# A decoder block with 64 experts: list entries spread over partitions, one weight load issued later, and one PSUM copy moved from ScalarE to VectorE

## What is computed

```python
g_idx = argmax(hn @ w_group + b_group)             # one group of 8
top_l, top_i = top_k(e_logits_of_group, 2)         # two of its 8 experts
w = softmax(top_l) * g_prob[g_idx]
# for each token t and each of its two experts e = g_idx * 8 + top_i:
hb = silu(hn[t] @ w_gate[e]) * (hn[t] @ w_up[e])   # 1024 -> 256
out[t] += w * (hb @ w_down[e])                     # 256 -> 1024
```

## Time and profile before

| | us |
|---|---|
| timed runs | 2643.99, 2638.89, 2644.9 |
| profiled execution | 2639.34 |
| its span | 2637.7 |
| TensorE busy | 2459.3 (93%) |
| VectorE busy | 1841.3 (70%) |
| ScalarE busy | 1049.5 (40%) |
| GpSimd busy | 518.3 (20%) |
| experts' stage, from its table load to the end | 1895.9 to 2637.7 |

### The profile page before, as it was taken

How to read it: one execution, slowest core, us unless ns; L and a number is a source line. 1 busy time by engine, 2 the same in 40 slices (tenths; PEclk the granted TensorE clock), 3 DMA queues, 4 the chain that set the end, 5 groups by cost and what they waited for, 6 DMA issues and landing times. The chain is left out here.

```text
span 2637.7 us, 33454 instructions
## 1 busy us (share of the span) xinstructions
PE 2459.3 (93%) x12296; PEld 2006.0 (76%) x12296; DVE 1841.3 (70%) x2387; ACT 1049.5 (40%) x1516; POOL 518.3 (20%) x474
## 2 busy tenths in 40 slices
PE   6999999999999999999995997999399999999998
PEld 6899888999877878889884775778277777766664
DVE  7699998677211068888886775466578888877773
ACT  5101101444212158788774221233255555544440
POOL 1222222111101101111110000011424443332221
PEclk9999999999999999999997998999699999999999
DMA  5111212223324153354424775546479999998886
GB/s 170 40 56 56 73 51 86 78 91 116 108 97 121 48 147 98 98 156 115 119 81 126 205 228 167 201 155 228 155 278 363 366 374 360 359 352 340 340 315 206
DMA packets 180271, 469.84 MB, mean 178 GB/s; under 512 B 33573, under 2 KB 104579, under 8 KB 145548
## 3 DMA queue, kind: packets, MB, share of 16 engines
q1 hardware_dynamic: 133202, 371.64, 41.3%
q0 software_dynamic: 31120, 49.48, 5.5%
q10 hardware_dynamic: 15794, 46.67, 4.6%
HBM read 408.65 MB, written 118.29 MB: 200 GB/s over the span
## 5 line engine op out<-in xcount | busy, mean ns | idle before, releaser
L92 PE MATMUL project_bank<-project_xnT_hi,project_w_hi 128*128 128x512 f32 (+4 forms) x1352 | 512.9, 379 | 0.8 <-DVE project_work L775 0.7
L93 PE MATMUL project_bank<-project_xnT_lo,project_w_hi 128*128 128x512 f32 (+4 forms) x1352 | 499.9, 370 | 0.0
L94 PE MATMUL project_bank<-project_xnT_hi,project_w_lo 128*128 128x512 f32 (+4 forms) x1352 | 497.7, 368 | 0.0
L788 DVE SCALAR_TENSOR_TENSOR project_work<-project_work,project_taps 128x2048 f32<-128x2048 f32 x128 | 335.3, 2620 | 4.5
L92 PEld LDWEIGHTS project_bank<-project_xnT_hi,project_w_hi 128*128 128x128 f32 (+1 forms) x1352 | 252.1, 186 | 36.7 <-issue 8.3
L93 PEld LDWEIGHTS project_bank<-project_xnT_lo,project_w_hi 128*128 128x128 f32 (+1 forms) x1352 | 252.2, 187 | 33.2 <-issue 6.8
L94 PEld LDWEIGHTS project_bank<-project_xnT_hi,project_w_lo 128*128 128x128 f32 (+1 forms) x1352 | 252.3, 187 | 27.2 <-issue 0.6
L2633 PE MATMUL experts_y_bank<-weights_down,experts_hT 128*128 128x512 f32 x544 | 246.9, 596 | 19.4 <-DMA weights_down<-in_w_down_dram 18.7
L1265 DVE TENSOR_TENSOR attend_pT<-attend_t_bank,attend_pT 128x512 fp32r<-128x512 f32 (+3 forms) x352 | 213.8, 613 | 33.7 <-ACT attend_pT L1199 32.7
L1132 PE MATMUL attend_o_bank<-attend_pT,attend_values 128*128 128x256 f32 x1216 | 225.0, 304 | 6.7 <-DVE attend_pT L1265 6.7
L1199 ACT ACTIVATE attend_pT<-attend_t_bank 128x512 fp32r<-128x512 f32 (+3 forms) x352 | 184.7, 540 | 86.9 <-PE attend_t_bank L1118 84.2
(11 more groups left out here) (311 smaller groups left out, 4620.7 us busy)
## 6 DMA issues: line engine op xcount, KB each, us to landing
weights_down<-in_w_down_dram SPq DMA_DIRECT2D x68, 1024.0 KB, 20.9
weights_gate_up<-in_w_gate_dram SPq DMA_DIRECT2D x45, 1024.0 KB, 7.2
weights_gate_up<-in_w_up_dram SPq DMA_DIRECT2D x45, 1024.0 KB, 18.8
weights_third<-in_w_gate_dram SPq DMA_DIRECT2D x23, 1024.0 KB, 7.1
weights_third<-in_w_up_dram SPq DMA_DIRECT2D x23, 1024.0 KB, 17.7
project_w_raw<-in_w_in_dram SPq DMA_DIRECT2D x36, 512.0 KB, 4.1
qk_d<-project_work SPq DMA_DIRECT2D x16, 1032.0 KB, 5.6
gate_d<-project_work ACTq DMA_DIRECT2D x16, 1024.0 KB, 4.1
```

The lines of the kernel that those rows point to most:

```text
L92: pe.matmul(out, lhs[0], rhs[0], start=first, stop=False)
L93: pe.matmul(out, lhs[0], rhs[1], start=False, stop=False)
L94: return pe.matmul(out, lhs[1], rhs[0], start=False, stop=last)
L788: nc.vector.scalar_tensor_tensor(out=work[:, 2, 0:SEQ], in0=work[:, 1, META - 1 + q:META - 1 + q + SEQ], scalar=taps[:, bass.ds(ct, 1), q] ...
```

## The change

It has three parts.

1. The table's entries are laid over the partitions in another order, both in the table load and in the loads of the further jobs' lists. Entry r went to partition r; now it goes to partition (r mod 16) x 8 + floor(r / 16). A list of 43 tokens, which filled partitions 0 to 42, now fills two or three partitions of each group of eight.
2. Gate and up of job 3 are no longer loaded at the end of route, but at the start of the experts' stage, behind the first gather and ahead of job 4's.
3. In the steps of jobs 0 to 61 `take_hidden` moves from ScalarE, where it stood between the halves of `split_high`, to VectorE, where it stands behind `scale_rows` and ahead of both halves of `split_low`. Job 62 and the jobs behind it keep it on ScalarE.

```diff
@@ stage_route, SyncE
             first_weights.load_down(sp, room_of(2), expert_of(2))
-            wait(sp, first_weights.low_ready, 4 + 2)
-            first_weights.load_gate_up(sp, 0, expert_of(3))
             for s in stored:
@@ stage_experts
+        def spread(entries):
+            return entries.rearrange("(b a) e o -> a b e o", a=16)
@@ SyncE
-            sp.dma_start(table[:, :, :], table_rows[0:P, :, :]).then_inc(table_loaded, 16)
+            sp.dma_start(table[:, :, :], spread(table_rows[0:P, :, :])).then_inc(table_loaded, 16)
@@ SyncE, load_list
-                sp.dma_start(columns[:, j + 1:j + 2, :], table_rows[bass.ds(first, P), bass.ds(n, 1), :],
+                sp.dma_start(columns[:, j + 1:j + 2, :], spread(table_rows[bass.ds(first, P), bass.ds(n, 1), :]),
@@ SyncE
             wait(sp, rows_loaded[room_of(0)], 16)
+            load_gate_up(3)
             load_gate_up(4)
@@ ScalarE, step
-                if before >= 1:
-                    take_hidden(n - 1, 1 - b)
-                if n >= 1 and after >= 1:
                     high_gate_up(n + 1, 1 - b, q + b, 1)
@@ VectorE
+            def take_hidden(n, b):
+                wait(dve, hidden_turned, n + 3)
+                wait(dve, down_done, n + 1)
+                nc.vector.tensor_copy(hT[:, b, :, :], gu_bank[:, b, 0:DE].rearrange("p (c t) -> p c t", t=P))\
+                  .then_inc(hT_ready, 1)
@@ VectorE, step, behind lower_x and scale_rows
+                if before >= 1:
+                    take_hidden(n - 1, 1 - b)
+                if after >= 1:
                     if n >= 1:
                         lower_gate_up(n + 1, 1 - b, 0)
                         lower_gate_up(n + 1, 1 - b, 1)
```

## The result

| | before | changed kernel |
|---|---|---|
| median of the runs, us | 2642.91 (2638.89 to 2644.9, 4 runs) | 2626.56 (2626.27 to 2628.89, 4 runs) |
| profiled execution, us | 2639.34 | 2628.89 |
| its span, us | 2637.7 | 2627.3 |

The ratio of the times is 0.9939, 95% interval 0.9924 to 0.9955: 16 us faster, 12 to 20. A second timing of the changed kernel, on another chip, gave 2629.54 us and a ratio of 0.9949 (0.9932 to 0.9966).

A forecast was written before the change was run, and what follows sets the result against it. TensorE, then late the fullest DMA engine, was taken as the bound. -14.0 (order), 0 (load) and +1.0 (copy) gave -13.0 us, execution 2626.3; with the runs' median offset 2631, so the middle, 2628.5, was named; range 2614 to 2644.

The forecast's parts named there:

- The bound: Experts' stage: TensorE sets the pace for some 40 jobs, then the fullest DMA engine; 18.7 us of TensorE waits.
- The dealing in fours: List gathers and scatters: engine j takes partitions 4j to 4j + 3 and 32 + 4j to 35 + 4j.
- Rival A: Lists' rows are dealt in eights, so the new order levels all engines and 18.7 us go: 2618 to 2625; chance 0.10.
- B: Experts' stage: memory's rate, not the DMA engines, is the limit, so time stays at 2639 to 2644; chance 0.16.
- the term of the sum, 5.1 us left to show: Experts' stage: after the new order, 20.3 us of backlog less 15.2 hidden by the loads' lead leave 5.1 us.
- The prediction's own lower case: Job-by-job tally of the experts' stage with weights at 7.4 us: 6.6 us of waits left, gain 12.
- the 14.0 of the term: Experts' stage: gain in us from the new entry order, TensorE's 18.7 us of waits falling to 4.7.
- Rival D: Start of the experts' stage: job 3's weights come late, 5 us given back, 2633; chance 0.04.
- The forecast of 1 us: Late steps: the copy of `hT` on VectorE delays the down product by 1.1 us, paid once; 1 us loss.
- rival C: VectorE's queue: `hT` waits behind a scatter's buffer and a gather, 1.1 us in each of 21 late steps: 2650; chance 0.12.
- What would show it: Signs: down-weight waits about 5 us from near job 50, scatter landing 8 to 9 us, seven or eight engines ending job 5's gather.
- T: Experts' stage: rows dealt in fours, the fullest engine builds a backlog, costing TensorE time once the loads' lead is used up.

The follow-up runs named there:

- level: Kernel before, table loaded by four DMAs so that list entry r goes to DMA engine r mod 16 by the map in fours: 2610.9 us, ratio 0.9874.
- packed: Kernel before, table loaded by four DMAs so that each DMA engine gets eight neighbouring list entries before the next gets any: 2661.33 us, ratio 1.0065.
- level_late: Kernel before, with only the lists of jobs 32 to 63 dealt entry r to engine r mod 16: 2615.74 us, ratio 0.9895.
- load_only: Kernel before, with only job 3's gate and up load moved into the experts' stage: 2645.84 us, ratio 1.0000.
- copy_only: Kernel before, with only the copy of `hT` moved from ScalarE to VectorE behind `scale_rows`: 2642.51 us, ratio 0.9998.
- no_copy: Changed kernel with the copy of `hT` back on ScalarE, keeping the new entry order and the later load: 2628.38 us, ratio 0.9932.
- level_early: Kernel before, with only the lists of jobs 0 to 31 dealt entry r to engine r mod 16: 2632.35 us, ratio 0.9958.
- level_all: `level` plus job 3's load in the experts' stage and the copy of `hT` on VectorE: 2611.26 us, ratio 0.9876.

## Why the prediction was right

**The bound.** Right. TensorE sets the pace up to some point, the fullest DMA engine behind it. That the engine is full, and neither memory nor the order of instructions, is shown by `level` and `packed`, which differ in nothing but the partition, and with it the engine, that each row goes to. No run tells the engine apart from something else that its group of partitions might share.

**The dealing in fours.** Right, and shown three times: by the gather of 43 rows at 0.41 and at 0.88, by `level` with no wait left, and by `packed` with 32.1 us. Rival A is dead with it: in eights, the changed kernel would have had no waits. The Trainium skill ("DMA: Bandwidth & Descriptors", The descriptor swizzle) gives this map for a plain transfer; here the gathers and scatters of lists behave as it says. The Trainium skill ("DMA: Bandwidth & Descriptors", Specifications) also has 8 partitions per engine as the convention. The prediction took this for eight neighbours, which would have forecast A; the page doesn't say which eight, and the map in fours has eight per engine as well. The Trainium skill ("DMA: Bandwidth & Descriptors", Specifications) has about 358 GB/s for one core, which would have forecast B; the 382 GB/s of `level`, for 100 us, are over that, with this one core at work.

**The size of part 1.** The step that was off is the term of the sum, 5.1 us left to show. 9.4 us did in idle time of TensorE (8.9 of it ahead of the down product), and the waits begin at 2381, step 2 + 449 / 10.08 = 46, and in the second execution 8 steps sooner, not near job 50. The prediction's own lower case, weights at 7.4 us per engine and job and so a smaller lead, gave 6.6 us and fits better. A second term was too small on the other side: idle time is not all that a late step costs. By the loss defined above, before has 24.5 us and not 18.7, after 12.8 to 15.2 and not 9.4 to 10.9. These 3 to 6 us are spent where the rows of TensorE don't call it idle, and they grow with the lateness: 0.6 us in `level_late`, 11 in `packed`. Ends of matmuls are modelled, so where exactly they go is open. The two errors offset in part: the gain of 24.5 - 12.8 = 11.7 us in the stretch stands against the 14.0 of the term. That is one execution against one, and the execution before was a fast one; by the ratios of the medians the spread alone brought 21 us and the whole change 16 and 13. So the size is known to be 12 to 21 us and no better, and that the sum met it within 2 us is in part luck.

**Part 2.** Right at 0: `load_only` 1.0000, and ScalarE took job 3's weights at 1932.50 without a wait for a DMA. Rival D is dead.

**Part 3.** The forecast of 1 us fits, but isn't proved. The mechanism of rival C is there, `hT` does wait behind a scatter's buffer in each late step, but its price of 1.1 us for each late step, 23 us, is excluded: `copy_only` 0.9998. Beside the spread a cost of some 5 us stays open, as said above. The expectation that waits of TensorE for VectorE's copy "of several us in total" would prove C was a bad test. There are 8.9 us of them, and they took the place of waits of the same size (11.3 us in `no_copy`). All of a step's inputs are late together when the engine is, and the one that is last by some tenths gets the label.

**The sum and its base.** 2628.5 was named; the median is 2626.56. The profiled span fell by 10.4 us, the median by 16. The 10.4 are 11.7 in the stretch of the loss and 1.2 behind it, less the 2.5 us by which that stretch begins later in the changed kernel's execution. Where it begins scatters. SyncE's load of the table, the first thing that the experts' stage does, in the kernel before:

```profile
1895.89 1.37 DMA experts_table<-table_d
```

In the two executions of the changed kernel it is issued at 1897.11 and, in the second one:

```profile
1890.35 0.57 SPq L2440 DMA_DIRECT2D experts_table<-table_d  x1
```

It is the same kernel twice, and it comes to this load 6.8 us apart; the whole second execution has a span of 2620.8 us against 2627.3. So the stages ahead, which no part of the change touches but for one load, brought some 7 us of scatter between these two executions, and a difference of two spans holds it twice. The choice of the middle between 2626.3 and 2631 was thus no better than this scatter allows.

**What would show it.** Waits for down weights fell to nothing, not to 5 us, since the label moved. The scatter's landing was forecast to fall to 8 to 9 us and fell from 9.9 to 9.6; 8.5 is reached only by `level`. A short list's rows still stand on few engines, and by T a scatter lands when its fullest engine is done. The last windows of job 5's gather have 6.6, 6.2 and 1.8 engines at once on average, not seven or eight, and none of them has over eight, as A would. VectorE has 62 more instructions, where 61 copies were named, and the copy takes 0.41 us.

## What to carry to other kernels

The rows of an indirect DMA here went to engines by their partition, in fours: partitions 4j to 4j + 3 and 32 + 4j to 35 + 4j, one set of eight engines for each half of 64 (3.2 engines at the end of 43 rows in order, 14 at once when dealt by this map). If lists are shorter than 128, put entry r on a partition of engine r mod 16, and count the rows of the fullest engine, not the mean share. An engine that is over its share runs up a backlog that shows long after, so a stretch without waits can still be worth 11 us (`level_early`); and the releaser that a late step names is the last of several, so take the sum of waits and not their names as the finding. Take neither from one execution: kernels of equal time differed by up to 6 us in loss and by up to ten steps in where the waits began.

## What the runs showed of the hardware

- With the rows levelled, one core moved 382 GB/s over 100 us at a mean share of 0.99 of its 16 engines. Before, the same window had 339 GB/s at 0.88, while TensorE waited.
- Four DMAs for the table in place of one cost 1.4 us: from their issue to the first `scale_rows` 8.58 us pass (1894.61 to 1903.19) in place of 7.19 (1895.89 to 1903.08); `level_all` has 8.73, the changed kernel with its one DMA 7.35. `level` is the fastest kernel all the same.
- Moving a 0.41 us copy between engines or a load across a barrier changed the label on 20 us of waits twice and their sum by 3 us or so, with no change of the median time beyond its interval.
